# Second expert's weight panels issued from ScalarE's queue, first expert's from SyncE's

## What is computed

```
def hierarchical_moe(h, w_router_group, w_router_expert, w_gate, w_up, w_down):
    ...
    group_logits = (t @ w_router_group).astype(jnp.float32)
    ...
    top_logit, top_local = lax.top_k(in_group, TOP_K)          # TOP_K = 2
    gate = jax.nn.softmax(top_logit, axis=-1) * p_group
    expert_id = g_sel[:, None] * EXPERTS_PER_GROUP + top_local # 64 experts
    ...
    def expert_block(args):
        xb, e = args
        hid = jax.nn.silu(xb @ w_gate[e]) * (xb @ w_up[e])
        return hid @ w_down[e]
```

## Time and profile before

| | us |
|---|---|
| median of 3 runs (1,539.18 to 1,542.05) | 1,541.14 |
| the profiled execution, by its own timer | 1,541.4 |
| its span in the trace | 1,539.5 |
| TensorE busy (95% of the span) | 1,460.3 |
| VectorE busy (36%) | 557.4 |
| ScalarE busy (29%) | 452.9 |
| SyncE's queue: 484.16 MB, share of the 16 DMA engines | 79.4% |

### The profile page before, as it was taken

The page is one execution under the profiler, slowest core; times in us unless marked ns, Lnnn a source line. Parts: engine busy times, 40 slices in busy tenths (PEclk is TensorE's granted clock), DMA queues, the critical chain, the costliest instruction groups (busy, mean ns, idle before and its releaser), DMA issues.

```text
span 1539.5 us, 20591 instructions
## 1 busy us (share of the span) xinstructions
PE 1460.3 (95%) x7899; PEld 896.0 (58%) x7899; DVE 557.4 (36%) x860; ACT 452.9 (29%) x763; POOL 71.0 (5%) x78
## 2 busy tenths in 40 slices
PE   7999999999999999999999988988988989999997
PEld 5998988888889977643444333333433433444342
DVE  5755877753676868411111111110111111111112
ACT  5434555533555685311111110110110111111112
POOL 1000000000030064200000000000000000000000
PEclk9999999999999999999999999999999999999999
DMA  9564346554544335999999999999999999999996
GB/s 317 182 219 165 112 159 212 195 196 159 191 148 155 115 133 187 411 422 418 415 422 422 422 422 422 422 422 422 421 422 422 422 422 422 422 422 415 422 421 256
DMA packets 107375, 491.87 MB, mean 319 GB/s; under 512 B 9447, under 2 KB 11635, under 8 KB 60212
## 3 DMA queue, kind: packets, MB, share of 16 engines
q1 hardware_dynamic: 105460, 484.16, 79.4%
q0 software_dynamic: 1504, 6.37, 1.2%
q10 hardware_dynamic: 352, 0.54, 0.1%
HBM read 508.82 MB, written 1.10 MB: 331 GB/s over the span
## 4 chain that ended last, share of the span: by engine, by line
PE 71%; DMA 21%; DVE 3%; POOL 2%; ACT 1%; issue 1%; SPq 1%; ACTq 0%; DVEq 0%
PE banks L1056 26%; PE banks L1572 21%; DMA slots<-in_w_up_dram 20%; PE banks L1607 9%; PE banks L1122 4%; PE banks L1516 3%; PE banks L1526 2%; PE banks L1123 2%; POOL areas L571 2%; SPq L457 1%; DVE w_split L1713 1%; PE banks L1046 1%; DVE xeT L2264 0%; PE banks L1154 0%; ACT heT L977 0%
## 5 line engine op out<-in xcount | busy, mean ns | idle before, releaser
L1572 PE MATMUL banks<-slots,xeT 128*64 128x512 f32 x1536 | 353.3, 614 | 40.6 <-DMA slots<-in_w_up_dram 40.6
L1572 PEld LDWEIGHTS banks<-slots,xeT 128*64 128x64 f32 x1536 | 111.9, 141 | 276.9 <-issue 214.1
L1607 PE MATMUL banks<-slots,heT 128*64 128x512 f32 x1024 | 226.8, 595 | 8.0 <-ACT heT L977 8.0
L1713 DVE TENSOR_TENSOR w_split<-raw,w_split 128x2048 fp32r<-128x2048 f32 (+2 forms) x96 | 206.1, 2175 | 70.8 <-ACT w_split L647 70.7
L647 ACT ACTIVATE w_split<-raw 128x2048 fp32r<-128x2048 f32 (+2 forms) x96 | 171.0, 1814 | 56.5 <-PE banks L1056 54.3
L1056 PE MATMUL banks<-h_both,w_split 128*128 128x256 f32 x1488 | 185.9, 285 | 0.0
L1056 PEld LDWEIGHTS banks<-h_both,w_split 128*128 128x128 f32 x1488 | 181.2, 193 | 2.5 <-issue 1.0
L2273 DVE TENSOR_TENSOR h_e<-banks,h_e 128x512 f32<-128x512 f32 x32 | 22.1, 692 | 421.3 <-PE banks L1572 421.3
L1607 PEld LDWEIGHTS banks<-slots,heT 128*64 128x64 f32 x1024 | 70.7, 137 | 145.2 <-issue 130.7
L1056 PE MATMUL banks<-w_split,h_both 128*128 128x512 f32 (+1 forms) x624 | 145.5, 390 | 3.1 <-DVE h_both L1703 2.4
L1056 PEld LDWEIGHTS banks<-w_split,h_both 128*128 128x128 f32 x624 | 113.6, 191 | 28.1 <-issue 4.7
(11 more groups left out here) (357 smaller groups left out, 1434.0 us busy)
## 6 DMA issues: line engine op xcount, KB each, us to landing
slots<-in_w_up_dram SPq DMA_DIRECT2D x128, 1024.0 KB
slots<-in_w_down_dram SPq DMA_DIRECT2D x128, 1024.0 KB
areas<-in_w_gate_dram SPq DMA_DIRECT2D x64, 1024.0 KB, 17.3
slots<-in_w_gate_dram SPq DMA_DIRECT2D x64, 1024.0 KB
raw<-in_w_in_dram SPq DMA_DIRECT2D x42, 1024.0 KB, 5.9
raw<-in_w_ff_dram SPq DMA_DIRECT2D x32, 1024.0 KB, 5.3
raw<-in_w_out_dram SPq DMA_DIRECT2D x12, 1024.0 KB, 5.0
raw<-in_w_ple_gate_dram SPq DMA_DIRECT2D x4, 1024.0 KB, 5.6
```

The costliest lines, as they stand in the source:

```text
L1572: last = mm(bank[SLOTS * e:SLOTS * e + SLOTS, :], xeT[:, k, odd, SLOTS * e:SLOTS * e + SLOTS], expert_panel(w, e, odd)[:, k, :], start=(k ...
L1607: last = mm(banks[half][SLOTS * e:SLOTS * e + SLOTS, :], heT[:, c, SLOTS * e:SLOTS * e + SLOTS], expert_panel("down", e, odd)[:, c, 512 * ...
L1713: last = tt(lo, source, hi, ALU.subtract)
```

## The change

SyncE's `load` gets a list of members: in the loop it issues the first expert's two transfers of each panel alone. Only the loads ahead of the loop (`gate`, `up`, `down` of pair 0, `gate` of pair 1) stay with SyncE for both experts. The second expert's two transfers go to ScalarE's queue by a new function `second_panel`, which is called at three points of ScalarE's `experts`: `gate` after the Silu, `up` after the copy to `heT`, `down` after the copies to `y_hi`. At each point ScalarE loads the expert's count into a register, waits for the whole of the panel's last use (both halves), and issues half 0 and half 1. The wait for `marks_done` is moved ahead of ScalarE's first pair, since the counts must be there.

```diff
-            def load(w, i, pair, odd, beyond):
+            def load(w, i, pair, odd, beyond, members=(0,)):
...
-                tokens = [None if beyond is None else tokens_of(pair, e) for e in range(2)]
+                tokens = [None if beyond is None else tokens_of(pair, e) for e in members]
...
-                    for e in range(2):
+                    for e in members:
...
             for w in ("gate", "up", "down"):
-                load(w, 0, 0, 0, None)
-            load("gate", 1, 1, 1, None)
+                load(w, 0, 0, 0, None, (0, 1))
+            load("gate", 1, 1, 1, None, (0, 1))
...
+            def second_panel(w, couple, at, odd, beyond):
+
+                weights, used, ahead = {"gate": (w_gate, gated, 2), "up": (w_up, upped, 1), "down": (w_down, downed, 1)}[w]
+                i, pair, parity = 2 * couple + odd + ahead, 2 * at + odd + ahead, (odd + ahead) % 2
+                tokens = act.value_load(count_i[0:1, bass.ds(2 * pair + 1, 1)], min_val=0, max_val=S)
+                act.wait_ge(used, 2 * (2 * couple + odd) + 2)
+                rows = 2 if w == "down" else 4
+                for half in range(2):
+                    part = slice(rows * half, rows * half + rows)
+                    act.dma_start(expert_panel(w, 1, parity)[:, part, :],
+                                  weights[0, 2 * pair + 1].rearrange("(p k) n -> p k n", p=P)[:, part, :],
+                                  cond=tokens > beyond).then_inc(pair_landed["odd_gate" if w == "gate" and parity else w, half], 16)
...
                 act_(h_e[:, :], banks[2][:, :], ACT.Silu).then_inc(silu_ready, 1)
+                if not last_couple:
+                    second_panel("gate", couple, at, odd, beyond)
...
                 act_(heT[:, :, :].rearrange("p c s -> p (c s)"), banks[2][:, :], ACT.Copy).then_inc(heT_ready, 1)
+                if not closing:
+                    second_panel("up", couple, at, odd, beyond)
...
                     act_(to, banks[half][:, :], ACT.Copy, scale=gate_of_slot).then_inc(ye_a, 1)
+                if not closing:
+                    second_panel("down", couple, at, odd, beyond)
...
-            experts(0, 0, first=True)
-            experts(0, 1)
             act.wait_ge(marks_done, 1)
+            experts(0, 0, 0, 0, first=True)
+            experts(0, 1, 0, 0)
```

More of the change, by code:

```diff
@@ L495, in _ @@
                     for w in ("gate", "up", "down"):
-                        load(w, r * PAIRS, 0, 0, r * SLOTS)
-                    load("gate", r * PAIRS + 1, 1, 1, r * SLOTS)
+                        load(w, r * PAIRS, 0, 0, r * SLOTS, (0, 1))
+                    load("gate", r * PAIRS + 1, 1, 1, r * SLOTS, (0, 1))
                     rest_of_pass(r * PAIRS, r * SLOTS)
@@ L964, in gather, with experts @@
                 act_(xeT[:, 4 * half:4 * half + 2].rearrange("p k o s -> p (k o s)"), banks[bank][:, :], ACT.Copy).then_inc(xe_a, 1)
-            def experts(couple, odd, first=False, last=False):
+            def second_panel(w, couple, at, odd, beyond):
[9 more added lines that the diff above has]
+                                  cond=tokens > beyond).then_inc(pair_landed["odd_gate" if w == "gate" and parity else w, half], 16)
+            def experts(couple, odd, at, beyond, first=False, last=False, last_couple=False):
                 i = 2 * couple + odd
@@ L991, in experts @@
                     act_(to, banks[half][:, :], ACT.Copy, scale=gate_of_slot).then_inc(ye_a, 1)
+                if not closing:
+                    second_panel("down", couple, at, odd, beyond)
             gather(0, 0)
             gather(0, 1, 2)
-            experts(0, 0, first=True)
-            experts(0, 1)
             act.wait_ge(marks_done, 1)
+            experts(0, 0, 0, 0, first=True)
+            experts(0, 1, 0, 0)
             fullest = act.value_load(count_i[0:1, NE:NE + 1], min_val=0, max_val=S)
             with act.Fori(1, PAIRS // 2 - 1) as j:
[L1000 to L1003, removed]
+                experts(j, 0, j, 0)
+                experts(j, 1, j, 0)
+            experts(PAIRS // 2 - 1, 0, PAIRS // 2 - 1, 0, last_couple=True)
+            experts(PAIRS // 2 - 1, 1, PAIRS // 2 - 1, 0, last=True, last_couple=True)
             with act.If(fullest > SLOTS):
@@ L1008, in _ @@
                     with act.Fori(0, PAIRS // 2 - 1) as j:
[L1009 to L1012, removed]
+                        experts(r * (PAIRS // 2) + j, 0, j, r * SLOTS)
+                        experts(r * (PAIRS // 2) + j, 1, j, r * SLOTS)
+                    experts(r * (PAIRS // 2) + (PAIRS // 2 - 1), 0, PAIRS // 2 - 1, r * SLOTS, last_couple=True)
+                    experts(r * (PAIRS // 2) + (PAIRS // 2 - 1), 1, PAIRS // 2 - 1, r * SLOTS, last=True, last_couple=True)
                 load_roots()
```

## The result

The changed kernel takes 1546.42 us in the median of seven runs (1544.38 to 1549.33), the kernel before 1541.14 in seven (1539.18 to 1542.79). The ratio is 1.0037, with a 95% interval of 1.0027 to 1.0046: slower by 5.3 us, where 5.2 were forecast. The profiled execution of after took 1544.38 us, the fastest of its seven, with a span of 1542.6.

What follows compares the result with a forecast made beforehand. The prediction took the expert loop to be paced by DMA bytes up to 1,248 us, then by TensorE. It added 2.4 us (empty queue) and 2.8 us (order of bytes) to 1,541.4 us: 1,546.6 us, range 1,539 to 1,555.

Runs made afterwards that it cites:

- run 3: Only the second expert's `up` panel goes through ScalarE, SyncE issues the rest, against the kernel before: 1551.66 us, ratio 1.0067.
- run 6: Second expert's `up` issued by idle GpSimd behind TensorE's marks, SyncE issuing the rest, against the kernel before: 1544.98 us, ratio 1.0024.
- `up` and `down` alone: Two kernels, each with only that panel of the second expert on ScalarE, against the kernel before: 1551.66 us for `up`, 1552.18 us for `down`.

## What to carry to other kernels

Where one queue already fills the DMA engines, its order of issue is a schedule: the panel needed first gets all the bytes. A second queue took half of them while both had work, however little it held, so before splitting loads, work out how far each queue can run ahead of the other when the consumer needs one panel from both, and price that lead at the full rate. Look also for places further on where the queue, having fetched ahead, runs empty: the last panels pay for those. What a split costs doesn't follow from the size of what is moved: here it was 2.3 us of loop for the `gate` panels, which are fetched two pairs ahead, 11.0 for `up`, 12.6 for `down`, and 5.4 for all three. And compare two traces by counting bytes up to one wait: surplus bytes and empty time tell order and lateness apart, where the totals of waits (40.6 us in the earlier trace rows, 44.8 after) only say that there is more.

## What the runs showed of the hardware

- ScalarE's queue issues a DMA that stands behind an ACTIVATE while that ACTIVATE still runs: at 718.15 us, 0.41 us ahead of the end of the second copy to `y_hi`, and 0.1 to 0.4 us ahead in every pair of after's timeline (behind `h_e` and `heT` of pair 3 it stands 0.35 and 0.22 us after their ends). So a transfer on that queue that must follow the result would need a wait of its own.
- The count load on ScalarE, seen once with 473 ns in before, takes 278 ns in the median of 92 in after. Its rows there, and those of the new issues:

```profile
L969 ACTq TENSOR_LOAD <-count_i x92: 273/278/476, 649.3 to 1506.7; - x92
...
L974 ACTq DMA_DIRECT2D slots<-in_w_up_dram x62: 339/339/342, 658.5 to 1500.2; - x62
```

- An issue on ScalarE's queue takes 339 ns in the median, 342 at most for `up` and 404 for `gate`, where SyncE's reached 2,467 ns for `gate` with everything in its one queue.
- Two busy queues share by halves: SyncE and ScalarE moved 1.25 and 1.29 MB in 6 us (run 3), SyncE and GpSimd 1.76 and 1.61 MB in 8 us (run 6). The sum was what one queue moves alone.

What stays open: the half transfer of surplus that is there without a lead, and a run that shows by itself how the late dips of `up` and `down` alone turn into the 6.7 and 5.0 us of the last pair.
